# The expert gathers of a product-key layer: a written-out list of GpSimd instructions becomes loops, and each row index is first copied to a fixed place

## What is computed

```python
q = (xb @ w_query).reshape(PEER_BLOCK, PEER_HEADS, 2, PEER_QDIM // 2)
s = jnp.einsum('thpd,hpnd->thpn', q, sub_keys)
sv, si = lax.top_k(s, PEER_TOPK)
...
idx = jnp.take_along_axis(cidx, pos, axis=-1)
gate = jax.nn.softmax(top_s.astype(jnp.float32), axis=-1)
act = jax.nn.gelu(jnp.einsum('thkd,td->thk', expert_u[idx], xb).astype(jnp.float32))
return jnp.einsum('thk,thkd->td', (gate * act).astype(xb.dtype), expert_v[idx])
```

## Time and profile before

| | |
|---|---|
| median of 3 runs | 2162.88 us (2159.51 to 2164.7) |
| the profiled execution | 2164.7 us, its span 2162.9 us |
| mean granted TensorE clock | 0.972 of full speed |
| busy in the span | PE 1732.3 us, VectorE 1122.1 us, GpSimd 735.3 us, ScalarE 268.6 us |
| moved | 723.14 MB, mean 334 GB/s |

### The profile page before, as it was taken

How to read it: one execution, slowest core, us unless ns; L and a number is a source line. 1 busy time by engine, 2 the same in 40 slices (tenths; PEclk the granted TensorE clock), 3 DMA queues, 4 the chain that set the end, 5 groups by cost and what they waited for, 6 DMA issues and landing times.

```text
span 2162.9 us, 14674 instructions
## 1 busy us (share of the span) xinstructions
PE 1732.3 (80%) x4545; PEld 786.5 (36%) x4545; DVE 1122.1 (52%) x1856; ACT 268.6 (12%) x629; POOL 735.3 (34%) x577
## 2 busy tenths in 40 slices
PE   6989999999879898677777777777777777777786
PEld 1133634455534587422222222222323222222232
DVE  0126778333334557465664665664565565564434
ACT  0120000211310200110110110110110110110111
POOL 1001000000000013345555555555555555555532
PEclk9989999999989899899999999999999999999998
DMA  7987778432177459699999999999999999999996
GB/s 275 328 298 259 275 274 306 168 112 78 60 289 292 156 201 369 260 405 423 410 407 423 414 414 423 412 416 423 414 414 423 407 417 422 417 411 423 422 378 257
DMA packets 144199, 723.14 MB, mean 334 GB/s; under 512 B 10121, under 2 KB 10329, under 8 KB 77090
## 3 DMA queue, kind: packets, MB, share of 16 engines
q0 software_dynamic: 92784, 614.83, 70.4%
q1 hardware_dynamic: 51216, 107.78, 14.0%
q10 hardware_dynamic: 162, 0.08, 0.0%
HBM read 720.52 MB, written 2.13 MB: 334 GB/s over the span
## 4 chain that ended last, share of the span: by engine, by line
DMA 42%; PE 38%; POOL 6%; DVE 6%; issue 6%; ACT 1%; DVEq 0%; ACTq 0%; SPq 0%
DMA ring<-in_expert_v,acc 24%; PE ps L684 11%; DMA ring<-in_expert_u,acc 10%; PE ps L874 8%; POOL ring L353 6%; PE ps L810 5%; PE ps L847 4%; DMA ring<-in_w_mod 3%; PE ps L632 3%; PE ps L678 3%; DMA ring<-in_w_query 2%; DMA ring<-in_w_out 1%; PE ps L737 1%; DMA ring<-in_w_in 1%; PE ps L654 1%
## 5 line engine op out<-in xcount | busy, mean ns | idle before, releaser
L874 PE MATMUL ps<-ring,wg 128*128 128x512 f32 x2000 | 925.2, 607 | 319.8 <-DMA ring<-in_expert_v,acc 319.7
L1242 DVE SCALAR_TENSOR_TENSOR ring<-ring,A 128x2048 f32<-128x2048 f32 x256 | 583.2, 2292 | 498.7 <-DMA ring<-in_expert_u,acc 490.6
L874 PEld LDWEIGHTS ps<-ring,wg 128*128 128x128 f32 x2000 | 363.4, 191 | 881.4 <-issue 479.2
L353 POOL DMA_INDIRECT ring<-in_expert_v,acc x256 | 367.8, 1437 | 398.3 <-PE ps L874 355.6
L353 POOL DMA_INDIRECT ring<-in_expert_u,acc x256 | 322.6, 1260 | 307.4 <-DVE ring L1242 173.6
L684 PE MATMUL ps<-ring,H 128*128 128x512 f32 x512 | 228.1, 605 | 5.6 <-DMA ring<-in_w_in 4.4
L574 ACT ACTIVATE wg<-K,VX 128x128 f32<-128x128 f32 x250 | 97.0, 400 | 1090.3 <-PE ps L874 892.1
L903 DVE SCALAR_TENSOR_TENSOR acc<-ring,vec,acc 128x512 f32<-128x512 f32 x240 | 180.5, 752 | 12.7 <-DMA ring<-in_w_mod 4.3
L303 POOL DMA_DIRECT2D ring<-in_w_mod x32 | 28.5, 891 | 402.2 <-DVE acc L903 293.6
L684 PEld LDWEIGHTS ps<-ring,H 128*128 128x128 f32 x512 | 97.8, 193 | 132.6 <-issue 125.2
L632 PE MATMUL ps<-ring,vec 128*2 128x512 f32 x256 | 116.1, 611 | 22.1 <-DMA ring<-in_w_mod 22.0
(11 more groups left out here) (206 smaller groups left out, 905.8 us busy)
## 6 DMA issues: line engine op xcount, KB each, us to landing
ring<-in_w_mod POOLq DMA_DIRECT2D x32, 2048.0 KB, 8.9
ring<-in_w_mod SPq DMA_DIRECT2D x16, 2048.0 KB, 8.0
ring<-in_w_in SPq DMA_DIRECT2D x16, 2048.0 KB, 8.2
ring<-in_w_out SPq DMA_DIRECT2D x8, 2048.0 KB, 8.1
ring<-in_w_query SPq DMA_DIRECT2D x8, 2048.0 KB, 16.7
ring<-in_expert_u,acc POOLq DMA_INDIRECT x256, 16.3
ring<-in_expert_v,acc POOLq DMA_INDIRECT x256, 15.8
B<-in_ctx SPq DMA_DIRECT2D x2, 1024.0 KB, 11.0
```

Source lines behind the costliest of these rows:

```text
L353: nc.gpsimd.indirect_dma_start(ring[:, slot, :], None, table, bass.IndirectOffsetOnAxis(ap=eidx[:, rank:rank + 1], axis=0)).then_inc(loade ...
L874: ins = mm(ps[:, 4 * b + n, :], diag[:, s, :], ring[:, s, n * CH:(n + 1) * CH], start=False, stop=False, skip_group_check=True)
L1242: v.scalar_tensor_tensor(out=ring[:, 4 + s, :], in0=ring[:, 4 + s, :], scalar=1.0, in1=A[:, b, :], op0=ALU.mult, op1=ALU.mult, accum_out=d ...
```

## The change

GpSimd's list of gathers becomes loops on the engine. An indirect DMA takes the address of its index column as a constant; so in a loop each gather first copies its column of `eidx` (128 x 1) to one of eight fixed columns (`slot_idx`, in a part of `wg` that is no longer used), by a `tensor_copy` on GpSimd that raises a new semaphore, `copied`; GpSimd waits for it, issues a no-op, and then the indirect DMA, which reads the fixed column. The semaphore values to wait for are now computed from the loop counters. The order of the gathers, and the slot that each waits for, stay as they were. The wait for `picked` stands where it stood in the order: the main loop over heads is cut into two halves, with that wait between them.

```diff
+        slot_idx = wgf[:, 4 * P:4 * P + 8].bitcast(U32)
...
-            def gather(table, slot, rank, loaded):
+            def gather(table, slot, rank, index, count, loaded):
+                nc.gpsimd.tensor_copy(index, eidx[:, bass.ds(rank, 1)]).then_inc(S["copied"], 1)
+                pool.wait_ge(S["copied"], count)
+                pool.nop(nofuse=True)
                 nc.gpsimd.indirect_dma_start(
-                    ring[:, slot, :], None, table,
-                    bass.IndirectOffsetOnAxis(ap=eidx[:, rank:rank + 1], axis=0)
+                    ring[:, slot, :], None, table, bass.IndirectOffsetOnAxis(ap=index, axis=0)
                 ).then_inc(loaded, 16)
 
-            def gather_u(r):
-                if r % TOPK == 0:
-                    pool.wait_ge(S["picked"], r // TOPK + 1)
-                pool.wait_ge(S["u_free"], r + 1)
-                gather(expert_u[0], 4 + r % 4, r, u_ld[r % 4])
-
-            def gather_v(r):
-                pool.wait_ge(S["pair_free"], r + 1)
-                gather(expert_v[0], r % 4, r, v_ld[r % 4])
+            def gather_u(rank, s, count):
+                pool.wait_ge(S["u_free"], rank + 1)
+                gather(expert_u[0], 4 + s, rank, slot_idx[:, s:s + 1], count, u_ld[s])
+
+            def gather_v(rank, s, count):
+                pool.wait_ge(S["pair_free"], rank + 1)
+                gather(expert_v[0], s, rank, slot_idx[:, 4 + s:5 + s], count, v_ld[s])
+
+            def pairs(q, u_rank, done):
+
+                for s in range(4):
+                    gather_u(u_rank + s, s, done + (2 * s + 1))
+                    gather_v(u_rank + (s - LAG), s, done + (2 * s + 2))
...
-            for r in range(LAG):
-                gather_u(r)
+            hq = TOPK // 8
+            for head, quad, end in ((0, 0, TOPK // 4), (1, TOPK // 4, LAG // 4)):
+                pool.wait_ge(S["picked"], head + 1)
+                with pool.Fori(quad, end) as q:
+                    for s in range(4):
+                        gather_u(q * 4 + s, s, q * 4 + (s + 1))
             pool.wait_ge(S["w_free"], 48)
-            for r in range(LAG, ranks):
-                gather_u(r)
-                gather_v(r - LAG)
-            for q in range(TAIL_QUADS):
+            with pool.Fori(1, TB * PH - 1) as g:
+                with pool.Fori(0, hq) as q:
+                    pairs(q, g * TOPK + q * 4 + TOPK // 2, g * (2 * TOPK) + q * 8 + (LAG - 2 * TOPK))
+                pool.wait_ge(S["picked"], g + 2)
+                pool.nop(nofuse=True)
+                with pool.Fori(0, hq) as q:
+                    pairs(q, g * TOPK + q * 4 + TOPK, g * (2 * TOPK) + q * 8 + (LAG - TOPK))
+            with pool.Fori(0, hq) as q:
+                pairs(q, q * 4 + (ranks - TOPK // 2), q * 8 + (2 * ranks - LAG - TOPK))
+            with pool.Fori(0, TAIL_QUADS) as q:
                 for s in range(4):
                     if s == TAIL_SLOT:
                         pool.wait_ge(S["tail_free"], q + 1)
                     else:
                         pool.wait_ge(S["pair_free"], q * 3 + (TAIL_RANK + TAIL_PE.index(s) + 2))
-                    gather(expert_v[0], s, q * 4 + (TAIL_RANK + s), v_ld[s])
+                    gather(expert_v[0], s, q * 4 + (TAIL_RANK + s), slot_idx[:, 4 + s:5 + s],
+                           q * 4 + (2 * ranks - LAG + s + 1), v_ld[s])
```

More of the change, by code:

```diff
@@ L194, in build @@
         keys_ready q_free score_psum score_ready u_free pair_free dots_ready gelu_done wgt_ready
-        diag_ready tail_free ssq3 std3 final_ready stored dve act""".split()
+        diag_ready tail_free copied ssq3 std3 final_ready stored dve act""".split()
         S = {n: sem(n) for n in names}
```

## The result

| | before | after |
|---|---|---|
| median | 2161.2 us (2158.38 to 2164.7, 4 runs) | 2315.02 us (2307.59 to 2316.02, 4 runs) |
| span of the profiled execution | 2162.9 us | 2306.0 us |

The ratio is 1.0696, with a 95% interval of 1.0672 to 1.0720: 7.0% slower. (The ratios aren't the quotients of the two medians, which lie up to some 0.2% beside them; differences in us are those of the medians.) The forecast was 2214 us with a range up to 2290; the direction is right, and the size lies outside.

A forecast was written before the change was run, and what follows sets the result against it. Transfers were taken to bound the expert part, their queue running dry once per head. 2164.7 us (profiled execution) + 45.5 after the picks + 5.5 in the tail = 2215.7, less 1.8 to the median: 2214 us, range 2160 to 2290.

The forecast's parts named there:

- (a): The copy of an index column on GpSimd, 512 times: 0.15 us each, bounds 0.10 and 0.29.
- (b): On GpSimd, from the copy's end to the gather's descriptor work: 0.65 us, plus 0.05 for the copy's own start.
- 0.2 us more than the 0.65: Sign that the prediction is wrong: computed waits between copy and gather on GpSimd costing this much more than assumed.
- (c): GpSimd's copy is held by VectorE's running product, as the gather is: a second point where VectorE can hold it.
- The term after the pick: Gathers after each of 13 picks lag 2.2 to 5.4 us; 3.5 taken, 45.5 us in all, bounds 0 and 78.
- The calm part: Each head away from its pick: four held points per pair take 2.66 of 2.67 us, so cost 0.
- the formula of the prediction: Calm part without GpSimd's idle cover: a pair takes 2.29 + 2.66 us plus twice any excess over (b).
- The tail: Last rounds, TensorE waiting for v rows: one GpSimd issue in each of five to six rounds, +5.5 us, bounds 0 and 10.
- The start: First 24 u rows, issued while TensorE still does the query projection, which ends later: cost 0.
- What is moved: Order of gathers, wait for `picked` and SP's queue: nothing moved past another DMA, cost 0.
- The rival "faster": If the written-out list's three long GpSimd gaps are code fetching, loops avoid them: 2152 us, chance 0.08.
- The rival "GpSimd becomes the bound": Four held points no longer fit in 2.67 us, each pair pays the excess twice: typically 2290 us, chance 0.2.

The follow-up runs named there:

- list_split: Kernel before with VectorE's pick cut in two in the loops over heads 2 to 13, first part before the product of rank 12: 2150.89 us, ratio 0.9952.
- list_sum: Kernel before with VectorE's product of two SBUF operands replaced by a sum over the u row alone: 2149.92 us, ratio 0.9947.
- list_copy_no_nop: Written-out list of before with the copy and the wait for it in front of each gather, but no no-op: 2183.71 us, ratio 1.0113.
- list_copy_ahead: Written-out list of before with copy, wait and no-op, each copy issued one gather ahead to its own column: 2174.95 us, ratio 1.0051.
- list_copy_free: Written-out list of before with a copy before each gather that nobody waits for, no no-op; gathers read `eidx`: 2173.7 us, ratio 1.0050.
- list_memset: Written-out list of before with a one-column memset, its wait and the no-op before each gather; gathers read `eidx`: 2182.52 us, ratio 1.0114.
- list_copy: Written-out list of before with copy, wait and no-op in front of each gather, constants throughout, no loops: 2311.34 us, ratio 1.0675.
- loop_sum: Changed kernel with VectorE's product of two SBUF operands replaced by a sum over the u row alone: 2158.92 us, ratio 0.9992.
- loop_fixed: Changed kernel's loops and no-op without the copy and its wait; gathers read the first eight index columns: 2168.42 us, ratio 1.0027.

## Why the prediction was wrong

**What bounded before: right.** The transfers, with a queue that ran dry after each pick; list_split agrees with it, and list_sum adds that the held gathers were the other half.

**(a) The copy, 0.15 us:** 0.19 measured. **(b) The way from copy to gather, 0.65 and 0.05 us:** 0.77 measured. Together with the gather's own 0.96 for 0.94, 1.93 us instead of 1.79 from gather to gather. That is inside the bounds of 1.34 to 2.53. The prediction named "0.2 us more than the 0.65" as the sign that it is wrong; by its own margin of 0.01 us this sign was too wide, and 0.14 us more per gather was enough.

**(c) The copy is held: right.** 2.08 us in place of 0.19 after the pick. Of the 995.6 us that copies and gathers take (334.9 + 333.4 + 327.3), 512 x (0.19 + 0.96) = 589 would be undisturbed; 407 us are holding. Before it was 690.4 - 512 x 0.94 = 209 (367.8 and 322.6 us on the page of before). The Trainium skill's rule ("SBUF — State Buffer", "Who interferes with whom") holds here in both halves: the copy, which reads SBUF, is held (2.08 us), the memset, which only writes, is not (112 ns), and beside a VectorE instruction of one SBUF operand neither the copy (191 ns) nor the gather (0.96 us) is.

**The term after the pick, 3.5 us x 13: somewhat large.** It is seen alone in list_copy_no_nop, whose calm part is whole. The starts of the first and of the last head with a pick before it, of the 13 in that kernel, and of the 13 in the kernel before:

```profile
944.22 2.18 POOL L358 COPY wg<-acc 128x1 uint32<-128x1 uint32 x1 [6.81 <-DVE ring L1248]
...
1942.53 2.18 POOL L358 COPY wg<-acc 128x1 uint32<-128x1 uint32 x1 [6.03 <-DVE ring L1248]
```

```profile
959.54 2.48 POOL L353 DMA_INDIRECT ring<-in_expert_u,acc  x1 [9.11 <-DVE ring L1242]
...
1927.39 2.75 POOL L353 DMA_INDIRECT ring<-in_expert_u,acc  x1 [8.22 <-DVE ring L1242]
```

998.31 / 12 = 83.19 us and 967.85 / 12 = 80.65 us: 2.5 us per pick, inside the 2.2 to 5.4 that the walk through the timeline gave. 13 x 2.5 = 33 us; over the whole kernel only 21 came of it, because some 13 came back at the start (below).

**The calm part, cost 0: this is the step that failed.** "It just fits": four held points in 2.66 us of the 2.67 that VectorE's product leaves. That was a result with no margin, worked out from a price that I had only bounded, and I entered it as 0. With the measured prices the four points take 0.96 + 0.97 + 0.96 = 2.89 us (0.19 and 0.77 from the start of the copy to that of the gather, 0.96 and the rounding back), 0.22 too many. By the formula of the prediction a pair then takes 2.29 + 2.89 = 5.18 us, 0.22 x 232 = 51 us more than before. It took more than that: in the changed kernel the first and the last of 12 such starts are these:

```profile
949.74 2.08 POOL L354 COPY wg<-acc 128x1 uint32 x1 [2.86 <-DVE ring L1261]
...
1953.31 2.08 POOL L354 COPY wg<-acc 128x1 uint32 x1 [3.41 <-DVE ring L1261]
```

They lie 1003.57 / 11 = 91.2 us apart, 10.6 us more than before. From the 49th gather to the 489th, the part with the picks and pairs, 1251.58 us pass (952.74 to 2204.32) instead of 1107.57 (959.54 to 2067.11): 144 us more. In the head shown, 32 gathers of 1.93 us are 61.8 us, the stop at the pick 3.4, and the rest of the 89.78, 24.6 us, is holding: 1.5 us per product, where the formula, with one gap of 0.96 us used in each product, would give 1.3. The formula supposes that the product always starts at the most useful moment. In fact it starts when a row lands (641.4 of the 649.6 us for which VectorE is idle before its products are waits for u rows). That this makes up the rest is argued, not tested.

**The sum over the runs.** What GpSimd has to do, from the pages (copies and gathers with their holding, and 512 times the gap before the gather), against 512 x 2.48 = 1270 us of transfers:

| kernel | GpSimd's work, us | time, us |
|---|---|---|
| before | 844 (gap 0.30) | 2161 |
| list_copy_ahead | 951 (0.15) | 2175 |
| list_copy_free | 987 (0.155) | 2174 |
| list_copy_no_nop | 1172 (0.27) | 2184 |
| list_memset | 1195 (0.77) | 2183 |
| list_copy | 1398 (0.77) | 2311 |
| after | 1390 (0.77) | 2315 |
| loop_sum (VectorE's sum in place of the product) | 987 (0.77) | 2159 |

Up to 1195 us of work the time stays between 2159 and 2184 us; at 1390 and 1398, above the 1270, it is 2311 to 2315. If GpSimd's excess (120 us) is paid in full, and with it the idle time at the picks (some 3.4 us each, 13 x 3.4 = 44 us), that is 164, of which 154 were measured. This is an account made afterwards, with one size of work above the threshold.

So the term of the sum that was mis-sized is the calm part: 0 predicted, and 110 to 130 us measured. list_copy and list_copy_no_nop, which differ by the no-op alone, lie 128 us apart; and the 144 us of the picks and pairs less 13 x 2.5 us for the picks are 111.

**The tail, 5.5 us: right.** From the 489th gather to the last 75.85 us pass (2204.32 to 2280.17) instead of 69.96 (2067.11 to 2137.07): 5.9 us more.

**The start, 0: not quite.** The 49th gather starts 6.8 us earlier than before (952.74, 959.54), and 12.6 us earlier in list_copy_no_nop (946.93). TensorE's query projection, before and after:

```profile
L847 PE MATMUL ps<-H,ring 128*128 128x256 f32 x512 | 116.3, 390 | 18.8 <-DMA ring<-in_w_query 18.4
```

```profile
L866 PE MATMUL ps<-H,ring 128*128 128x256 f32 x512 | 111.6, 380 | 2.2 <-DMA ring<-in_w_query 1.7
```

It waited 18.4 us for the weights `w_query` and now waits 1.7; in all five kernels with a copy before each gather and VectorE's product in place it is 0.9 to 3.2 us, in the nine others 12.2 to 22.6. The prediction kept the start at 0 because the projection ends after the first 24 u rows, and overlooked that these rows are fetched beside the weights. That slower gathers leave the weights more of the transfers is argued; no run tests it. **What is moved:** nothing to correct.

**The rival "faster":** wrong. The three long gaps of the list aren't due to the list. In before they stand in front of the 220th, the 326th and the 432nd gather. In loop_fixed they stand in front of the same three, the first and the last of them here:

```profile
1385.32 0.93 POOL L355 DMA_INDIRECT ring<-in_expert_v,acc  x1 [3.84 <-issue]
...
1921.03 0.94 POOL L355 DMA_INDIRECT ring<-in_expert_v,acc  x1 [5.17 <-issue]
```

They come every 106 gathers, written out or looped (in the kernel after, 3.35 us in front of the 114th, 220th, 326th and 432nd), so that the fetching of code is no likely reason; which it is stays open. **The rival "GpSimd becomes the bound":** right in kind, and it named the point from which it decides (0.01 us), but it got 0.2 as a chance. A threshold that lies 0.01 us from the estimate, with 0.5 us of uncertainty in the price, deserved about half.

## What to carry to other kernels

When a working queue hides an engine's own pace, add up that engine's work per unit of the bounding resource, with everything it is held by, and compare the two sums. If they are within 10% after the change, "it fits" is no zero: here 6% below (list_memset, 1195 us against 1270) cost 20 us, and 9% above (after, 1390) cost 154. An instruction that the same engine must wait for costs the round trip and not its own length; issue it one step ahead, or once for many, before thinking about anything else. And a second read of SBUF on GpSimd beside a VectorE that works on two SBUF operands isn't the 0.19 us of an undisturbed copy but up to the length of a whole VectorE instruction (2.31 us beside a product of 2.29).

## What the runs showed that I hadn't expected

- A no-op on GpSimd behind a wait that is met late costs 0.5 us (gap 0.77 against 0.27 us), and nothing where the wait is met already (0.30 and 0.30).
- The same round trip costs 149 us with two held points (list_copy), 20 us with one (list_memset, 0.11 us shorter per gather), and about 9 us with none (loop_sum against list_sum). The parts don't add up; the threshold between them does the work.
- The DMA share of a stretch reads 0.95 to 0.97 at 368 to 381 GB/s and 1.01 at 423. It says little about whether the transfers bound.
- A gap on GpSimd in front of every 106th gather, in lists and in loops: 3.6 to 4.0 us in before, 3.8 to 5.2 in loop_fixed, 3.35 in the kernel after.
- TensorE's granted clock is lower in the kernel after: 0.940 of full speed (2.4 GHz) as a mean of the profiled execution (0.972 before), 0.94 in the head shown (1.00 in that of the earlier trace rows). TensorE's matmuls for the rows took 649 ns instead of 607, and it waited 412.9 us for v rows instead of 319.7. GpSimd hardly waits for it any more (24.8 and 15.5 us), so that this isn't what costs the time. What lowered the clock isn't shown.
